# Two neighbouring 1 MB weight pieces per transfer in the experts' stage of a two-block fp32 kernel on Trainium2

## The reference, cut to what matters

```python
D_MODEL = 1024
D_FF = (7 * D_MODEL) // 2      # 3584
N_EXPERTS = 8
TOP_K = 2

def swiglu(h, w_gate, w_up, w_down):
    return (jax.nn.silu(h @ w_gate) * (h @ w_up)) @ w_down

def moe_ffn(h, router_w, router_b, w_gate, w_up, w_down):
    t = h.reshape(bsz * seq, d)
    logits = t @ router_w + router_b
    top_v, top_i = lax.top_k(logits, TOP_K)
    gates = jax.nn.softmax(top_v, axis=-1)
    combine = jnp.sum(jax.nn.one_hot(top_i, N_EXPERTS) * gates[..., None], axis=1)
    for e in range(N_EXPERTS):
        y_e = swiglu(t, w_gate[e], w_up[e], w_down[e])
        out = out + combine[:, e:e + 1] * y_e
```

## Time and profile before

| | us |
|---|---|
| median of 3 runs | 2362.04 |
| lowest and highest | 2360.24, 2364.8 |
| the profiled execution, its own time | 2365.51 |
| its span, from first to last instruction | 2363.8 |

### The profile page before, as it was taken

The page is one execution under the profiler, slowest core; times in us unless marked ns, Lnnn a source line. Parts: engine busy times, 40 slices in busy tenths (PEclk is TensorE's granted clock), DMA queues, the critical chain, the costliest instruction groups (busy, mean ns, idle before and its releaser), DMA issues.

```text
span 2363.8 us, 32498 instructions
## 1 busy us (share of the span) xinstructions
PE 2331.9 (99%) x11826; PEld 1966.9 (83%) x11826; DVE 1851.6 (78%) x1838; ACT 1446.0 (61%) x1494; POOL 70.2 (3%) x93
## 2 busy tenths in 40 slices
PE   8999999999999999999999999999999999999998
PEld 7888897788888888888888878887888888878887
DVE  7766677888888888888888986678766766687766
ACT  4544455777777777777777764456644644546544
POOL 1100000100000000000000000020000000100000
PEclk9999999999999999999999999999999999999999
DMA  7754554899999999999999955543455555442552
GB/s 260 263 191 184 193 178 170 327 382 375 384 380 382 379 381 378 382 378 382 378 383 390 393 207 193 195 146 118 143 192 184 186 193 195 172 136 100 193 184 101
DMA packets 88136, 610.68 MB, mean 258 GB/s; under 512 B 10140, under 2 KB 10172, under 8 KB 16892
## 3 DMA queue, kind: packets, MB, share of 16 engines
q1 hardware_dynamic: 83520, 595.10, 67.2%
q0 software_dynamic: 4112, 13.31, 1.5%
q10 hardware_dynamic: 432, 1.31, 0.1%
HBM read 598.15 MB, written 11.53 MB: 258 GB/s over the span
## 4 chain that ended last, share of the span: by engine, by line
PE 89%; DVE 6%; ACT 2%; DMA 1%; issue 1%; POOL 0%; ACTq 0%; DVEq 0%; SPq 0%
PE banks L1208 17%; PE banks L1264 9%; PE banks L1266 9%; PE banks L1270 9%; PE banks L1213 9%; PE banks L1285 8%; PE banks L1287 8%; PE banks L1286 8%; DVE lo L1920 2%; PE banks L1240 2%; PE banks L1591 2%; PE banks L1306 1%; PE banks L1621 1%; DVE acc L2453 1%; PE banks L1644 1%
## 5 line engine op out<-in xcount | busy, mean ns | idle before, releaser
L1920 DVE TENSOR_TENSOR lo<-raw,hi 128x2048 fp32r<-128x2048 f32 x547 | 1251.0, 2290 | 210.5 <-ACT hi L611 208.0
L611 ACT CAST hi<-raw 128x2048 fp32r<-128x2048 f32 x543 | 1038.4, 1913 | 230.1 <-PE banks L1270 101.2
L1208 PE MATMUL banks<-xhl,hi 128*128 128x512 f32 x1776 | 424.4, 391 | 4.5 <-DVE gsum L1969 3.9
L1208 PEld LDWEIGHTS banks<-xhl,hi 128*128 128x128 f32 x1776 | 328.9, 188 | 71.9 <-issue 4.8
L1285 PE MATMUL banks<-hi,xhl 128*128 128x512 f32 x896 | 354.1, 395 | 1.9 <-DVE lo L1920 1.7
L1287 PE MATMUL banks<-hi,xhl 128*128 128x512 f32 x896 | 349.7, 390 | 0.0
L1286 PE MATMUL banks<-lo,xhl 128*128 128x512 f32 x896 | 348.9, 389 | 0.0
L1264 PE MATMUL banks<-hi,hh 128*128 128x512 f32 x808 | 316.0, 391 | 0.1
L1266 PE MATMUL banks<-lo,hh 128*128 128x512 f32 x808 | 315.5, 390 | 0.0
L1270 PE MATMUL banks<-hi,hl 128*128 128x512 f32 x808 | 249.2, 390 | 0.0
L1213 PEld LDWEIGHTS banks<-xhl,lo 128*128 128x128 f32 x1776 | 228.3, 191 | 9.1
(11 more groups left out here) (394 smaller groups left out, 2412.4 us busy)
## 6 DMA issues: line engine op xcount, KB each, us to landing
raw<-in_moe_w_gate SPq DMA_DIRECT2D x112, 1024.0 KB, 5.0
raw<-in_moe_w_up SPq DMA_DIRECT2D x112, 1024.0 KB, 5.0
raw<-in_moe_w_down SPq DMA_DIRECT2D x112, 1024.0 KB, 4.8
raw<-in_ffn_w_gate SPq DMA_DIRECT2D x58, 1024.0 KB, 4.8
raw<-in_ffn_w_up SPq DMA_DIRECT2D x58, 1024.0 KB, 4.8
raw<-in_ffn_w_down SPq DMA_DIRECT2D x58, 1024.0 KB, 4.8
raw<-in_mix_pieces SPq DMA_DIRECT2D x46, 1024.0 KB, 4.8
g_rows<-zeros POOLq DMA_DIRECT2D x14, 256.0 KB, 10.5
```

The costliest lines, as they stand in the source:

```text
L611: nc.scalar.copy(hi[:, hslot(S, c), 0:n], raw[:, c % RING, 0:n]).then_inc(S.hi_done, 1)
L1208: pe.matmul(bank[b + s][:, :], hi[:, hr, a:a + P], xhl[:, k, :], start=(k == 0), stop=False, skip_group_check=True)
L1920: v.tensor_tensor(lo[:, c % RING, 0:n], raw[:, c % RING, 0:n], hi[:, hslot(S, c), 0:n].bitcast(F32), ALU.subtract).then_inc(S.lo_done, 1)
```

## The change

In the experts' stage SP no longer issues one transfer for each piece but one for each pair: `raw[:, slot:slot + 2, :]` is filled by one transfer of 2 MB whose source is two neighbouring pieces. The transfer waits until both pieces that held the two slots have been multiplied, and it increments the semaphore of the even slot alone. Both pieces of a pair therefore wait for the same count (`full_at`). Behind the stage, the counts of the odd slots are lower by the number of rounds that used no semaphore of their own. The order of the pieces, the ring, `hi`, `lo` and all products stay as they were; 168 transfers stand where 336 were. All other stages keep their transfers of one piece.

```diff
+        pairs = next((st["B"], st["B"] + 6 * STEPSW * NE) for st in stages if st["kind"] == "moe")
+        assert pairs[0] % RING == 0 and RING % 2 == 0
+
+        def full_at(S, c, i):
+
+            slot, loads = c % RING, c // RING + 1
+            if S is not main or pairs[0] <= c < pairs[1]:
+                slot -= slot % 2
+            elif c >= pairs[1] and slot % 2:
+                loads -= (pairs[1] - pairs[0]) // RING
+            return S.raw_full[slot], 16 * (loads + i)
...
                 def load(name, c, i, j):
-                    for r in range(2):
-                        sp_load(sp, S, c + r, i, w[name][e][:, bass.ds(2 * j + r, 1), :].rearrange("p j c -> p (j c)"), PIECE)
+                    if not isinstance(i, int) or c >= RING:
+                        sp.wait_ge(S.multiplied, c - RING + 2 + 6 * i)
+                    slot = c % RING
+                    sp.dma_start(raw[:, slot:slot + 2, :], w[name][e][:, bass.ds(2 * j, 2), :]).then_inc(S.raw_full[slot], 16)
...
         def act_hi(act, S, c, i, n=PIECE):
 
-            act.wait_ge(S.raw_full[c % RING], 16 * (c // RING + 1 + i))
+            act.wait_ge(*full_at(S, c, i))
...
             if part_no == 0:
-                act.wait_ge(main.raw_full[c % RING], 16 * (c // RING + 1))
+                act.wait_ge(*full_at(main, c, 0))
...
         def pe_raw_wait(pe, c):
 
-            pe.wait_ge(main.raw_full[c % RING], 16 * (c // RING + 1))
+            pe.wait_ge(*full_at(main, c, 0))
```

## The result

The changed kernel takes 2472.68 us (median of 4 runs, 2471.79 to 2475.56), the kernel before 2363.14 us (4 runs, 2360.24 to 2364.8). The ratio is 1.0464, with a 95% interval from 1.0451 to 1.0477: 109.5 us slower. The forecast was 2440 us, in a range from 2408 to 2482. The sign and the mechanism came out as forecast; the size was 78 us where it is 109.5.

The account below looks back on a forecast made before the run. PE was taken to set the pace, with transfers close behind. Waits for down pairs (66.2 us), first up pairs at borders (7.6) and late loads (4) summed to 77.8 us, on 2362.0 giving 2440 us, range 2408 to 2482.

Parts of the forecast that it names:

- PE bounds, nothing to win: Experts' stage: PE busy 937.25 of 938 us; 168 saved issues and fixed parts of transfers costed at zero.
- The later issue: SP's queue: a pair's load waits for the second old piece; gate pair issue moves from 707.49 to 710.20.
- The chain of R and its slack: Down pair must land within 5.87 us of issue; 1.38 us late, 48 waits, 66.2 us.
- R: The down pair of a step; its largest need, 1.38 us, lengthens a step from 16.82 to 18.20 us.
- G and U: The gate pair and up pair; needs of 0.79 and 0.71 us, covered by the down pair's wait.
- The wait for the first U of an expert: First up pair at the 7 expert borders: 1.08 us each, 7.6 us in all.
- The landing of a pair: Issue to landing of 2 MB: 7.25 us, with ends 7.05 and 7.8; between 7.0 and 7.8, chance 0.68.
- The transfers of 512 KB and late loads: Pairs pushed back 1.25 us, 14 times, and late loads in the last expert: bounded by 0 and 9, taken as 4 us.
- (a): Rival: a pair lands sooner, in 6.3 to 6.85 us; at 6.8 us, 49 us slower, 2411 us; chance 0.13.
- (b): Rival: not slower, the pair lands within 5.87 us, so 2362 us, no change; chance 0.05.
- (d): Rival: the long transfer is slower, landing in 8.2 us or more; 126 us, 2490 us; chance 0.08.
- (c): Rival: PE's waits also lower the granted clock, 90 us more, 2530 us; chance 0.06.

Follow-up runs that it names:

- the first experiment: Changed kernel with each pair as two 1 MB transfers issued together after the pair's wait, each with its own semaphore: 2372.24 us, ratio 1.0046.
- The down pairs alone: Changed kernel with 2 MB transfers for slots 2 and 3 only (down pieces of steps 0 to 5, first up pieces): 2471.91 us, ratio 1.047.
- the swap: Changed kernel with ACT's rounding of hidden values before the first down piece's `hi`, and DVE's `hl` before its `lo`: 2457.3 us, ratio 1.0404.

## Why the prediction was right, and where its size was off

**PE bounds, nothing to win.** Right. The saved issues and fixed parts gave nothing that can be seen, in any kernel. (The row of the DMA share was misread by one slice: it has eight tenths in slice 8 and nine in slices 9 to 23. Nothing rests on it.)

**The later issue.** Right in its place and its times: the first experiment has the pair issued as late and loses 11 us.

**The chain of R and its slack.** Right: the slack of 5.87 us, the need of R above those of G and U, and that the needs don't add. The down pairs alone make the whole loss. The wait for the first U of an expert is there too: 0.96 to 1.29 us at the seven borders, 1.14 as a mean, where 1.08 was forecast (1.52 by the same formula with the landing as measured). Taking `hl` off the chain lowers the wait by as much as its 0.7 us says.

**The landing of a pair.** This term was mis-sized. I took 7.25 us, 4.75 for the first MB and 2.5 for the second; it is 7.6 to 7.8. The 2.5 came from rows of a full queue. Two transfers of 1 MB issued together take 7.37, so a second MB costs 2.6 there, the later issue of its own transfer included; the 2 MB transfer adds 0.3, of which 0.2 goes away when its source is one run. The upper bound, 7.8, was from transfers of other sizes, and the truth was nearer to it. With 7.69 the sum's own formula gives R 1.82 us, as 18.66 - 16.82 = 1.84 us in the row and 1.79 as a mean of the four middle rows of the table. By the formula that makes 48 x 0.44 = 21 us more for R and 7 x 0.44 = 3 us for the first U.

**The transfers of 512 KB and late loads.** I took 4 us for all of them. With a landing of 7.69 us the waits for R and the first U make 12.4 us in each of experts 2 to 7, where 13.0 were measured: 3.5 us more in six experts, of which two falls of the clock are 3. The last expert, where loads ran late before the change already, lost 13.2 us where five waits for R make 9.1: 4 us more. So the 4 us came out as a sum, but by luck in its parts: nearly nothing for the transfers of 512 KB, and all of it in the last expert. In the changed kernel the gate pairs behind `gs` land 0.7 to 1.0 us late, less than my 1.25, and R's wait covers it for the most part; only where the swap took that wait away did it show.

**The stage's start.** The step that cost 7.7 us was in the sum with one wait for R alone. The queue is behind there in the kernel before already, and ACT's copy of the first down pair waited 5.89 us for its transfer:

```profile
443.14 1.90 ACT L625 CAST hi<-raw 128x2048 fp32r<-128x2048 f32 x1 [5.89 <-DMA raw<-in_moe_w_down]
```

I had used these rows for the price of a MB and did not ask what a later issue does where the queue has no lead. The first expert lost 17.3 us where its waits for R and the first U make 12.4. That made 5 us, some 3 of them a fall of the clock behind PE's wait of 5.48 us.

Together: 21 + 3 for the landing, 5 at the start and 3 for the clock in two other steps make 32, against 31.7 us that were missing.

**The rivals.** (a), a shorter landing, is out, and so is (b), in time after all. (d), the slow long transfer, was right in its direction: 0.3 us instead of the 0.95 that its 8.2 us needed, and its cause, the two runs of the source, has 0.2 of them. (c), the clock, came in for about 6 us: summed over stretches of 4 us, the granted clock lost 6.9 us in the stage, a part of it while PE was idle, and none before. It fell three times, each time to 0.50 of full speed, the lower of the two levels (1.2 of 2.4 GHz): behind PE's wait of 5.48 us at the start and behind waits of 1.82 and 1.84 us (the stretch from 846 to 850 us above, with 0.57, holds the last). It did not fall behind a wait of 2.02 us, nor behind any of those up to 1.77. So the remark against (c), that the waits are shorter, held for the usual wait, but with little to spare.

The advice of the Trainium skill ("DMA: Bandwidth & Descriptors", section "Rules for kernel authors") to use at least 1 MiB for each DMA says nothing for going beyond it here, and no run here gained from it. The formula of the Trainium skill's section "Anatomy of one DMA" on the same page, which is for transfers issued from GpSimd, gives an estimate of 6.8 us for a pair; these pairs are issued from SP and the traces have 7.6 to 7.8, so the measurement decides.

## What to carry to other kernels

One signal for a larger transfer delays the use of its first byte to the landing of its last, and its issue waits for the release of its last buffer; both must fit into the slack between the issue and the first use, which can be read from two rows, the issue and the start of the first reader. Where the buffers are few (here three pairs), the right question is not how busy the DMA engines are but how long one transfer takes against how long the other buffers last. If transfers are to be issued together anyway, keep a semaphore for each piece: here that recovered 98.6 of 109.5 us.

## What the runs showed of the hardware that I had not expected

A transfer of 2 MB whose source has two runs of 8 KB for each partition takes SP 0.37 us to issue and lands 7.69 us later; with one run of 16 KB it is 0.33 us to issue and 0.2 us less to land. That such a small detail moves the kernel by some 10 of the 15 us is due to the 48 places where it is on the path.

Waits of PE of 1.82 and 1.84 us were each followed by 3 to 4 us at 0.50 of the full clock, 1.7 us lost each time, while one of 2.02 us in the same trace was not. So near 2 us it was not the length of the wait alone that decided; what did is open.
